# One decoder step on one core: sample scores earlier in VectorE's order, selected and recent values on four column groups, memory's values as the stationary operand

## The reference, cut to what matters

```python
# A: sparse attention; 15 chosen blocks of 64 rows and the own row, and the last 512 rows and the own row
s_past = einsum('bqgrd,bqgkld->bqgrkl', qg, kv_sel[..., 0, :]) * scale      # selected
o_s = einsum(p[..., :n_past], kv_sel[..., 1, :]) + einsum(p[..., n_past:], slc[:, :, 1])
p_w = masked_softmax(einsum('bqgrd,bsgd->bqgrs', qg, kv_w[:, :, 0]) * scale, mw)
o_w = einsum('bqgrs,bsgd->bqgrd', p_w, kv_w[:, :, 1])                       # recent (window)
# B: forgetting attention over all 4096 past rows, 8 heads of 64
s_p = einsum('bqhd,bshd->bhqs', q, k_past) * scale + a_new + r_past
o = einsum('bhqs,bshd->bqhd', softmax(s_p), v_past)
# M: 4 heads of 128 over 256 memory rows
o_m = einsum('bhtm,bmhd->bthd', softmax(einsum('bthd,bmhd->bhtm', q, mk) * scale), mv)
# all: gates, z = branch @ w_branch, merged = sum(gate * z), y = rmsnorm(merged @ w_out) + x
```

## Time and profile before

| what | value |
|---|---|
| median of 3 runs | 1538.83 us (1530.58 to 1539.1) |
| the profiled execution | 1541.35 us, its span 1539.6 us |
| PE busy | 1275.1 us, 83% of the span |
| DVE busy | 804.4 us, 52% |
| the last stage | from 810.8 us to the end |
| its steps 1 to 6, each | 75.5 to 79.9 us |

### The profile page before, as it was taken

The page is one execution under the profiler, slowest core; times in us unless marked ns, Lnnn a source line. Parts: engine busy times, 40 slices in busy tenths (PEclk is TensorE's granted clock), DMA queues, the critical chain, the costliest instruction groups (busy, mean ns, idle before and its releaser), DMA issues. The chain is left out here.

```text
span 1539.6 us, 27628 instructions
## 1 busy us (share of the span) xinstructions
PE 1275.1 (83%) x10055; PEld 876.6 (57%) x10055; DVE 804.4 (52%) x1197; ACT 254.4 (17%) x714; POOL 169.7 (11%) x153
## 2 busy tenths in 40 slices
PE   1799844999999497998888996979696969797995
PEld 1788743887788474555547863545353536364342
DVE  2345112088999932456662556475747565735022
ACT  0101124101211201244441201010101001000113
POOL 0000000020000000000004040505050504030000
PEclk9999986999999755789999998989897989898898
DMA  8888025167888614100009368687868586756750
GB/s 218 258 254 259 22 101 181 57 205 223 274 292 287 198 37 179 55 1 1 1 1 316 88 213 284 187 284 230 284 217 275 186 292 210 251 177 217 272 217 29
DMA packets 206021, 282.08 MB, mean 183 GB/s; under 512 B 21933, under 2 KB 126918, under 8 KB 205438
## 3 DMA queue, kind: packets, MB, share of 16 engines
q1 hardware_dynamic: 110078, 202.47, 39.0%
q10 hardware_dynamic: 89376, 60.01, 13.6%
q0 software_dynamic: 6432, 17.83, 3.7%
HBM read 273.32 MB, written 11.11 MB: 185 GB/s over the span
## 5 line engine op out<-in xcount | busy, mean ns | idle before, releaser
L1594 PE MATMUL bank<-xnT,e_wg 128*128 128x260 f32 x1152 | 279.6, 401 | 0.7 <-DMA e_wg<-in_w_in 0.7
L1594 PEld LDWEIGHTS bank<-xnT,e_wg 128*128 128x128 f32 x1152 | 226.5, 199 | 80.5 <-issue 34.0
L598 PE MATMUL score_banks<-xnT,oT 128*128 128x260 f32 (+1 forms) x864 | 197.3, 386 | 8.3 <-DMA oT<-in_w_in 8.3
L1578 POOL DMA_INDIRECT d_slc<-in_cache_nsa_slc,selrow x128 | 150.3, 1174 | 428.5 <-PE score_banks L1661 384.8
L598 PEld LDWEIGHTS score_banks<-xnT,oT 128*128 128x128 f32 (+1 forms) x864 | 161.7, 189 | 38.3 <-DMA oT<-in_w_in 8.5
L234 PE MATMUL score_banks<-c_cols,c_w 64*64 64x64 f32 (+1 forms) x4096 | 131.7, 224 | 48.2 <-DMA c_w<-in_w_cmp 32.7
L234 PEld LDWEIGHTS score_banks<-c_cols,c_w 64*64 64x64 f32 x4096 | 128.5, 141 | 51.6 <-issue 51.5
L273 DVE COPY c_cols<-c_page 128x1024 f32<-128x1024 f32 x48 | 48.3, 1117 | 95.8 <-DMA c_page<-in_cache_nsa_cmp 82.6
L1602 PE MATMUL bank<-oT,e_wb 128*128 128x512 f32 x192 | 91.6, 621 | 8.2 <-DVE cst L1853 7.1
L1627 PE MATMUL bank<-d_vpage,d_pf 128*8 128x512 f32 x512 | 86.2, 686 | 13.8 <-DMA d_vpage<-in_cache_fox_kv 13.8
L1305 DVE TENSOR_REDUCE f_nm<-score_banks 128x2 f32<-128x512 f32 (+3 forms) x56 | 45.0, 803 | 79.2 <-PE score_banks L1256 78.4
(11 more groups left out here) (369 smaller groups left out, 1541.9 us busy)
## 6 DMA issues: line engine op xcount, KB each, us to landing
d_vpage<-in_cache_fox_kv SPq DMA_DIRECT2D x256, 256.0 KB, 4.3
d_kpage<-in_cache_fox_kv SPq DMA_DIRECT2D x96, 256.0 KB, 5.9
oT<-in_cache_fox_kv SPq DMA_DIRECT2D x80, 256.0 KB, 4.1
mt<-in_cache_fox_kv SPq DMA_DIRECT2D x80, 256.0 KB, 3.9
e_wg<-in_w_in ACTq DMA_DIRECT2D x36, 512.0 KB, 6.0
c_page<-in_cache_nsa_cmp SPq DMA_DIRECT2D x128, 128.0 KB, 3.6
oT<-in_w_in ACTq DMA_DIRECT2D x13, 1024.0 KB, 8.2
c_page<-in_cache_nsa_cmp ACTq DMA_DIRECT2D x64, 128.0 KB, 3.6
```

The source lines that it names most:

```text
L598: last = nc.tensor.matmul(pj[ch.n % 2][i][0:ch.w, 0:NM if ch.mem else TH], w[:, c, ch.off:ch.off + ch.w], rhs, start=c == 0, stop=c == DC - 1)
L1578: nc.gpsimd.indirect_dma_start(out=slc[:, n, :], out_offset=None, in_=k.cache_slc, in_offset=bass.IndirectOffsetOnAxis(ap=k.selrow[:, at:a ...
L1594: last = nc.tensor.matmul(gate_bank[n % 2][:, 0:TH], wg[product % WR][:, c, :], k.xnT[:, c, part * TH:(part + 1) * TH], start=c == 0, stop ...
```

## The change

Three things change. On VectorE both halves of the window scores come before the third key group, the memory scores move from the end of the row to the place behind them, and the selected rows' scores stand ahead of the fourth key group; the merges move with them. On TensorE the 30 products of `small_values` go in turn to four column groups of the array (output partitions 0, 32, 64 and 96), and the turning product for them adds the four parts, since its other operand is now `k.fold` (ones where the partition modulo 32 is the column) in place of the identity. Memory's values become the stationary operand: 8 products with one moving column write the turned result at once, so the four turning products of L1674 go, as does the copy at L1974; the copy into `k.om` stands in `small_sums` now. `small_values` gets two waits more, one for a buffer that is cleared once at the start, one for `place_sums` of an earlier step.

```diff
@@ -1429,8 +1429,8 @@
         qrow = sb("d_qrow", [P, 2, BRW])
-        fvs, mvs = sb("d_fvs", [P, BRW]), k.mvs
-        svs = k.svs
+        fvs = sb("d_fvs", [P, BRW])
+        svs = ybuf[:, 512:512 + 2 * G * HD].rearrange("p (i n) -> p i n", i=2)
         LATE, PER = (NB - EARLY) * GROUPS, 4
@@ -1495,7 +1495,7 @@
         om_turned = stat_bank[:, 3 * P + 16:3 * P + 16 + MH]
-        sv_bank, mv_bank = sum_bank[0:R, :], sum_bank[32:32 + MH, :]
+        sv_bank = sum_bank[:, 0:2 * G * HD]
         so_bank = sum_bank[:, 256:256 + 3 * NB * H]
@@ -1643,6 +1643,8 @@
                     te.wait_ge(p_done, b * 3 + 3)
+                    te.wait_ge(fv_zero, 2)
+                    after(te, placed, (b - 1) * 4)
                     te.wait_ge(slc_in, (b + 1) * 16 * NSLC)
@@ -1656,22 +1658,23 @@
                     for i, (cols, left, right) in enumerate(parts):
-                        nc.tensor.matmul(sv_bank[:, cols], left, right, start=i == 0, stop=i == len(parts) - 1, skip_group_check=True)
-                    for n in range(NMEM):
-                        last = nc.tensor.matmul(mv_bank[:, :], sm[:, n, :], mem[:, n, BRW:2 * BRW], start=n == 0, stop=n == NMEM - 1)
+                        at = 32 * (i % 4)
+                        nc.tensor.matmul(sv_bank[at:at + R, cols], left, right, start=i < 4, stop=i >= len(parts) - 4, skip_group_check=True)
+                    for h in range(MH):
+                        for n in range(NMEM):
+                            last = nc.tensor.matmul(om_turned[:, h:h + 1], mem[:, n, BRW + h * P:BRW + (h + 1) * P], sm[:, n, h:h + 1],
+                                                    start=n == 0, stop=n == NMEM - 1)
                     last.then_inc(small_free, 1)
...
                     te.wait_ge(os_out, b * 2 + 2)
-                    after(te, placed, b * 5)
+                    after(te, placed, b * 4)
                     for c in range(4):
...
                     for br in range(2):
-                        nc.tensor.matmul(ow_turned[:, br * R:(br + 1) * R], svs[:, br, :], k.ident[32:32 + R, 32:32 + R], start=True, stop=True)
-                    for c in range(MH):
-                        last = nc.tensor.matmul(om_turned[:, c:c + 1], mvs[:, c * P:(c + 1) * P], k.ident[32:32 + MH, 32 + c:33 + c], start=True, stop=True)
+                        last = nc.tensor.matmul(ow_turned[:, br * R:(br + 1) * R], svs[:, br, :], k.fold[:, 0:R], start=True, stop=True)
                     last.then_inc(sums_turned, 1)
@@ -1758,7 +1761,7 @@
                 y_products(1, 1)
-                te.wait_ge(placed, NB * 5)
+                te.wait_ge(placed, NB * 4)
                 nc.tensor.matmul(so_bank[:, 0:2 * NB * H], k.dupall, k.ow[:, :, :, :].rearrange("p i b h -> p (i b h)"), start=True, stop=True)
@@ -1970,8 +1973,8 @@
                     after(ve, sums_turned, b)
-                    nc.vector.tensor_copy(svs[:, :, :], sv_bank[:, 0:4 * HD].rearrange("p (i n) -> p i n", i=2)).then_inc(os_out, 1)
-                    nc.vector.tensor_copy(mvs[:, :], mv_bank[:, :]).then_inc(os_out, 1)
+                    nc.vector.tensor_copy(svs, sv_bank.rearrange("p (i n) -> p i n", i=2)).then_inc(os_out, 1)
+                    nc.vector.tensor_copy(k.om[:, :, b:b + 1], om_turned.unsqueeze(2)).then_inc(os_out, 1)
 
@@ -1982,7 +1985,6 @@
                                               ow_turned[rows, :].rearrange("p (i h) -> p i h", i=2)).then_inc(placed, 1)
-                    nc.vector.tensor_copy(k.om[:, :, b:b + 1], om_turned.unsqueeze(2)).then_inc(placed, 1)
 
@@ -2002,6 +2004,7 @@
                 nc.vector.memset(fv_bank[:, :], 0.0).then_inc(fv_zero, 1)
+                nc.vector.memset(sv_bank, 0.0).then_inc(fv_zero, 1)
                 ve.wait_ge(zero, 1)
@@ -2022,15 +2025,20 @@
                         query_row(kind, b)
-                    for i in range(3):
-                        for m in late[i + 1:i + 2]:
-                            page_scores(m)
-                        if i < 2:
-                            small_scores(b, "win", i)
-                        merge_until(b, 2 + i)
+                    for m in late[1:2]:
+                        page_scores(m)
+                    small_scores(b, "win", 0)
+                    small_scores(b, "win", 1)
+                    merge_until(b, 2)
+                    memory_scores(b)
+                    for m in late[2:3]:
+                        page_scores(m)
                     small_scores(b, "slc", 0)
+                    merge_until(b, 3)
                     small_scores(b, "slc", 1)
-                    memory_scores(b)
+                    merge_until(b, 4)
+                    for m in late[3:4]:
+                        page_scores(m)
                     merge_until(b, 5)
@@ -2161,9 +2169,8 @@
         k.oT = sb("oT", [P, 12, T])
-        held, k.slrow = sb("srow", [P, M_ALL]), sb("slrow", [NB, H])
-        k.srow, k.mvs = held[0:NB, :], held[32:32 + MH, 0:BRW]
-        k.svs = held[32:32 + R, BRW:BRW + 2 * G * HD].rearrange("p (i n) -> p i n", i=2)
+        held, k.slrow = sb("srow", [NB, M_ALL]), sb("slrow", [NB, H])
+        k.srow = held
         k.snew = sb("snew", [P, 3, NB, H])
```

## The result

The median fell from 1538.57 us (1530.58 to 1539.1, 4 runs) to **1491.22 us** (1485.38 to 1497.82, 4 runs): ratio 0.9697, 95% interval 0.9654 to 0.974. The forecast was 1485.6, range 1468 to 1512. The total came out 5.6 us above the forecast, well inside the range, but its parts did not: what was taken off TensorE gave half of what it was priced at, and the softmax part of the steps, where the clock held better, gave 9 us that were not in the sum. The rest of the text takes the two apart.

What follows compares the result with a forecast made beforehand. It took TensorE to set each step's pace until `small_sums`, then VectorE until TensorE's L1636; terms of 22.8 + 6.3 + 3.6 + 23.4 - 2.9 = 53.2 us off the median of 1538.8 gave 1485.6 us, range 1468 to 1512.

Steps and rivals of the forecast that it cites:

- A: `small_values` on four column groups: products take 1.0 us in place of 3.85, in 8 places, 22.8 us off.
- B: Four turning products fewer, ahead of `small_sums` in steps 2 to 6 and twice at the end: 6.3 us off.
- C: Copy behind `small_sums` gone from VectorE: 0.6 us a step in steps 1 to 6, 3.6 us off.
- D: VectorE's new order hides its waits for keys: 23.4 of 28.8 us off, ends 22.0 and 24.8.
- E: Step 7, without keys, pays: slot 3's merge now stands behind the first selected half; 2.9 us lost, ends 0 and -6.
- a rival with a chance of 0.15: TensorE's clock stays at 2.4 GHz around L1636 as idle time shrinks: 11 us more off, 1474; chance 0.15.
- The objection: Against the clock gain around L1636: shrunken waits come back in part as TensorE's waits for later merges; no size given.
- the signs that the prediction named: New profile: 60 records in about 1.0 us, earlier `small_sums`, one key wait of about 4 us, shorter steps 2 to 6.
- Two signs of being wrong: VectorE's first selected row waits for gathers in steps with keys; TensorE instead of VectorE ends last before L1636.
- Column groups give nothing at 64 columns: Rival for `small_values`: packing gains 0 at this size, so the time is 1505.5 us; chance 0.10.
- The transfers take over: Rival: key landings do not come earlier with TensorE; about 20 us of gains lost, 1506 us; chance 0.12.
- The gather blocks VectorE: Rival: the wait for 16 gathers, now ahead of the fourth key group, makes the kernel slower, 1560 us; chance 0.03.

Runs made afterwards that it cites:

- e3: The changed kernel with all products of `small_values` on the first column group; 1502.2 us, ratio 0.9769.
- e4: The changed kernel with the four own-row products of `small_values` put behind the 24 others; 1474.74 us, ratio 0.9588.
- e2: The changed kernel with VectorE's old order, so TensorE's part of the change alone; 1524.4 us, ratio 0.989.
- e1: The kernel before with VectorE's new order alone; 1500.64 us, ratio 0.975.
- e9: e4 with VectorE's merges of slots 3 and 4 ahead of the first selected half in steps without key groups; 1473.84 us, ratio 0.9597.
- e8: The kernel before with 28 useless products ahead of TensorE's wait for the maxima in every step; 1526.38 us, ratio 0.9925.
- e5: e4 with the copy of the small sums in two buffers, used in turn; 1471.46 us, ratio 0.9576.
- e10: e4 with the edits of e5 and e9, and memory's products moved behind the gate products; 1469.07 us, ratio 0.9547.

## Why the forecast held, and where its parts did not

**A and B, 29.1 forecast, 14.7 measured** (head 104.6 to 91.7, end 117.9 to 116.1). B is as sized: e3's head, without packing, is 15.0 us against 16.0 to 16.1. The step that failed is A's 1.0 us for the products. It took L897's records for the whole of `small_values`, and B's sentence "`small_values`' products with 128 rows and its own-row products were in one even stream" was wrong: an own-row product came 0.15 us behind its neighbour, where 56 ns is the rule. The 24 products with 128 rows do pack fourfold, so A is 1.9 us and not 2.85; e4 shows that the other 0.9 was in the order of the products. The rest of the gap in the steps is the clock: it fell behind `small_values` in steps 2, 3, 5 and 7, some 1.7 us a time. In the end, where the forecast let A and B pass whole, 1.8 us came; the clock is at 0.50 for 13.6 us there, but what that costs no run shows (e2's end, with 20.5 us at 0.50, took 115.4).

**C, 0.6 a step forecast, 0.8 measured.** In step 3 the first key group begins 0.41 us behind the start of `small_sums`, 1.16 before (1061.56 - 1060.40), and `place_sums` is some 0.09 shorter. Over steps 2 to 6 the scores take 199.3 us in the changed kernel and 203.4 in e1, which keeps the copy (and the rest of TensorE's part of before); steps 1 and 7 have other waits. In e2 it brought 0.5 in all seven: C counts only with D.

**D, 23.4 forecast.** The key waits went from 28.8 to 3.1 and the gathered rows took 4.0 back in step 1: 21.7. What stays in step 1, 2.8 for keys and 4.0 for the gather, is just over the 4.0 to 6.8 that were given; the gather there was not seen. It took 32 us from its first issue (886.0) to VectorE's first selected row (918.2), where the prediction worked with 28.

**E, -2.9 forecast.** Step 7's scores took 38.3 us, 36.4 before, so -1.9; -4.3 in e1. The mechanism is the one named, shown by e9. With 4.1 for C, 21.7 for D and -1.9 for E, 23.9 of the 24.6 us that the scores gained are placed.

**The softmax, 0 forecast, 8.8 measured.** The prediction had the mechanism and its price, 11 us, but as a rival with a chance of 0.15, as though it excluded the rest. It belonged in the sum: D and C shorten TensorE's wait, whatever else happens. e1 gives 11.0 for the order alone, e8 shows the cause. The size fits: 19.0 us less at half the clock (33.7 to 14.7) are 9.5 us, an estimate that takes TensorE as busy throughout. The objection, waits that come back for later merges, holds in part: TensorE's waits for merged values at L1602 grew from 8.1 to 20.0 us, while those for the maxima fell by 42.3.

So 53.2 met 49.1 (12.9 + 24.6 + 8.8 + 1.8, and 1.0 ahead of step 1's `small_values`) because A and B were 14.4 too large and the softmax 8.8 too small. That the total was right is partly luck.

Of the signs that the prediction named, the key waits came as forecast, `small_sums` did not (1.2 us sooner in step 3 and 2.9 in step 4, where 3.8 was expected). Steps 2 to 6 got shorter by 8.4, 5.4, 9.7, 10.3 and 6.7 us, 7 to 10 forecast, and step 7 by 1.1. Two signs of being wrong came up, each in a single step: VectorE's first selected row waits for the gathers in step 1, which has keys, and in step 7 TensorE ends last, with no wait ahead of L1636.

**The other rivals.** *Column groups give nothing at 64 columns* is refuted: e3 loses 11 us, and in e4 16 records of 64 columns begin within 0.23 us, four in 56 ns. The Trainium skill's rule, page "TensorEngine Tiling (Array Packing)", section Performance Considerations, against tiling for a dimension that is small already, does not hold for these products; the same section's advice to tile columns where the stationary operand has few of them (4 here) does. *The transfers take over* did not happen in the change. In e5 and e10 VectorE waits for keys again, 18.3 and 29.5 us, and the DMA engines' share in e10's step 3 is 0.90, 0.76 before; whether their rate or the order of SP's queue sets those waits was not tested. *The gather blocks VectorE* happens for 4.0 us in step 1 and in step 7, far from the point where it would decide.

## What to carry over

A wait that a reorder shortens can also change the clock of what stands behind it, 8.8 us here: that belongs in the sum, not among the rivals. Before you price packed products by the best-packed row, see whether the stream changes its number of rows, and put products with few rows together. Try a move together with its cover: the copy taken out of VectorE was worth 0.5 us while key waits stood behind it, and 4 once the order had hidden them.

## What was not expected of the hardware

- The clock fell to 1.2 GHz (granted 0.50) while TensorE was busy for 3.40 of 3.40 us, behind 4 us of packed products and products with one moving column. Where memory's products moved, the stretch moved with them. Whether the one-column products alone suffice stays open: e3, which has them unpacked, shows a stretch from some 7 us behind the start in two of seven steps.
- Products with one moving column and 128 stationary columns took 1.95 us for 16 records, some 0.12 us each, twice the 56 ns of those with 64 moving columns and 4 stationary ones.
- A change between 128 rows and 8 in TensorE's stream costs some 0.09 us; putting the products with few rows together took `small_values`' products from 1.92 to 1.01 us.
- 6.3 us of useless products in a step made the kernel 0.75% faster.
